# Matmuls of constants into an unused PSUM bank inside the recurrence stage of a two-block transformer kernel

## The reference, cut to what matters

```python
def _gla_scan(q, k, log_f, v, s0):
    ...
    def step(s, xs):
        qc, kc, gc, vc = xs
        a = jnp.cumsum(gc, axis=2)
        diff = a[:, :, :, None, :] - a[:, :, None, :, :]
        decay = jnp.exp(jnp.where(causal[:, :, None], diff, -jnp.inf))
        scores = jnp.sum(qc[:, :, :, None, :] * kc[:, :, None, :, :] * decay, axis=-1)
        o = jnp.einsum('bhts,bhsv->bhtv', scores, vc) + jnp.einsum('bhtk,bhkv->bhtv', qc * jnp.exp(a), s)
        a_last = a[:, :, -1:, :]
        s_new = jnp.exp(a_last[:, :, 0, :, None]) * s + jnp.einsum('bhsk,bhsv->bhkv', kc * jnp.exp(a_last - a), vc)
        return s_new, o
```

## Time and profile before

| what | value |
|---|---|
| runs | 3959.08, 3965.97 and 3971.05 us; median 3965.97 us |
| span of the profiled execution | 3950.7 us, 15.3 us less than the median of the runs |
| PE busy | 3628.5 us, 92% of the span |
| DVE busy | 2203.3 us, 56% |
| ACT busy | 1589.9 us, 40% |
| mean granted TensorE clock | 0.944 |
| chain that ended last, by engine | PE 81%, DVE 8%, ACT 5%, DMA 4%, issue 2% |

### The profile page before, as it was taken

The page is one execution under the profiler, slowest core; times in us unless marked ns, Lnnn a source line. Parts: engine busy times, 40 slices in busy tenths (PEclk is TensorE's granted clock), DMA queues, the critical chain, the costliest instruction groups (busy, mean ns, idle before and its releaser), DMA issues.

```text
span 3950.7 us, 52215 instructions
## 1 busy us (share of the span) xinstructions
PE 3628.5 (92%) x19934; PEld 2784.4 (70%) x19934; DVE 2203.3 (56%) x3277; ACT 1589.9 (40%) x2690; POOL 304.0 (8%) x398
## 2 busy tenths in 40 slices
PE   8998797999999687999999998999999999889998
PEld 7886465666788445456878766787877878667877
DVE  7866855897785784237762346665233332654332
ACT  3335744898423662113222336322233222453222
POOL 0110001110111002001210000111000001000001
PEclk9999568999999758999999999999999999999999
DMA  7551013998455005997773310575323223312222
GB/s 278 175 170 65 2 54 107 347 373 312 173 195 161 1 34 213 409 406 261 267 240 104 101 59 12 186 232 197 105 81 128 96 94 104 134 33 91 93 94 75
DMA packets 164958, 618.35 MB, mean 157 GB/s; under 512 B 18540, under 2 KB 20117, under 8 KB 163581
## 3 DMA queue, kind: packets, MB, share of 16 engines
q1 hardware_dynamic: 114928, 420.58, 29.6%
q0 software_dynamic: 45568, 166.75, 12.8%
q10 hardware_dynamic: 4238, 27.90, 1.8%
HBM read 595.95 MB, written 16.31 MB: 155 GB/s over the span
## 4 chain that ended last, share of the span: by engine, by line
PE 81%; DVE 8%; ACT 5%; DMA 4%; issue 2%; SPq 0%; ACTq 0%; POOL 0%; DVEq 0%; POOLq 0%
PE psum L2500 23%; PE psum L2513 12%; PE psum L843 12%; PE psum L928 5%; PE psum L995 4%; PE psum L2108 4%; DMA ring<-wtile 3%; PE psum L772 3%; PE psum L2339 2%; PE psum L1212 1%; PE psum L2127 1%; PE psum L2358 1%; PE psum L1222 1%; PE psum L780 1%; DVE spare L1318 1%
## 5 line engine op out<-in xcount | busy, mean ns | idle before, releaser
L796 ACT CAST small_r<-ring 128x1024 fp32r<-128x1024 f32 x263 | 275.0, 1048 | 1070.6 <-PE psum L843 336.6
L800 DVE TENSOR_TENSOR ring_r<-ring,small_r 128x1024 fp32r<-128x1024 f32 x264 | 322.8, 1225 | 677.4 <-ACT small_r L796 677.1
L796 ACT CAST PB_r<-ring 128x1024 fp32r<-128x1024 f32 x247 | 255.8, 1049 | 544.2 <-PE psum L2500 326.8
L800 DVE TENSOR_TENSOR ring_r<-ring,PB_r 128x1024 fp32r<-128x1024 f32 x248 | 299.5, 1222 | 247.8 <-ACT PB_r L796 247.4
L2500 PE MATMUL psum<-H_r,ring_r 128*128 128x512 f32 x1344 | 336.3, 392 | 0.0
L2500 PE MATMUL psum<-H_r,small_r 128*128 128x512 f32 x1344 | 326.9, 395 | 0.0
L2500 PE MATMUL psum<-H_r,PB_r 128*128 128x512 f32 x1344 | 318.7, 390 | 0.0
L2500 PEld LDWEIGHTS psum<-H_r,small_r 128*128 128x128 f32 x1344 | 252.4, 188 | 61.1
L2500 PEld LDWEIGHTS psum<-H_r,ring_r 128*128 128x128 f32 x1344 | 252.3, 188 | 55.9
L2500 PEld LDWEIGHTS psum<-H_r,PB_r 128*128 128x128 f32 x1344 | 252.4, 188 | 53.3
L843 PE MATMUL psum<-H_r,small_r 128*128 128x512 f32 (+1 forms) x1040 | 275.2, 368 | 0.1
(11 more groups left out here) (445 smaller groups left out, 6589.7 us busy)
## 6 DMA issues: line engine op xcount, KB each, us to landing
ring<-wtile SPq DMA_DIRECT2D x776, 512.0 KB, 5.3
spare<-wmod POOLq DMA_DIRECT2D x97, 512.0 KB, 4.8
H<-wmod POOLq DMA_DIRECT2D x48, 512.0 KB, 4.5
PB<-wmod POOLq DMA_DIRECT2D x48, 512.0 KB, 4.4
X<-wmod POOLq DMA_DIRECT2D x47, 512.0 KB, 4.9
PB<-wahead POOLq DMA_DIRECT2D x16, 512.0 KB, 7.5
h_rows<-PB POOLq DMA_DIRECT2D x10, 512.0 KB, 4.5
PB<-wmod SPq DMA_DIRECT2D x4, 1024.0 KB, 15.5
```

Of the source, the lines that this page charges most:

```text
L796: copy(high(j), slot(g0 + j)).then_inc(high_ready.sem, 1)
L800: nc.vector.tensor_tensor(low(g0 + j), slot(g0 + j), high(j).bitcast(F32), ALU.subtract).then_inc(low_ready.sem, 1)
```

## The change

A helper `filler` issues matmuls of `ones` against the first columns of `ident` and its neighbour, into bank 7, with no semaphore. It is called at five places on TensorE and nowhere else: 12 matmuls of 256 columns ahead of the first cell's wait, 9 ahead of the wait for the first cell's second piece, 9 ahead of the wait for the second cell; and in every unit of cells 0 to 3 and of units 0 to 3 of cell 4 (28 units) one of 256 columns ahead of `output` and one of 128 columns ahead of `contribution`. That is 86 matmuls in each layer, 172 in all. Nothing is removed, and no wait is added or taken away.

```diff
             def ten(eng):
+                def filler(count, width):
+                    for _ in range(count):
+                        nc.tensor.matmul(bank[7][:, 0:width], ones, cn("ident", 0, width), start=True, stop=True)
+
                 def scores(u):
                     c, v, ch, d, i = units[u]
+                    if (c, v) in ((0, 0), (0, 2), (1, 0)):
+                        filler(12 if v == 0 and c == 0 else 9, 2 * P)
                     if (c, v) == (0, 0):
                         eng.wait_ge(cell_ready.sem, b_ce + 1)
                     if (c, v) == (0, 2) or c and v == 0:
...
                     if u + 1 < n:
                         scores(u + 1)
+                    if c < 4 or (c == 4 and v < 4):
+                        filler(1, 2 * P)
                     output(u)
                     if u + 1 < n:
+                        if c < 4 or (c == 4 and v < 4):
+                            filler(1, P)
                         contribution(u + 1)
```

## The result

The changed kernel takes 4012.3 us (median of 4 runs, 4009.04 to 4017.21) against 3962.5 us for the kernel before beside it. The ratio of the runs is 1.0139, with a 95% interval of 1.0113 to 1.0166 (the two medians alone divide to 1.0126, inside it): slower, and the forecast of 4014 us lies 1.7 us off. The total hides two steps that went another way than foretold, and they cancel.

What follows compares the result with a forecast made beforehand. It took TensorE at 1.2 GHz to bound layer 0's recurrence, narrowly ahead of VectorE, and VectorE layer 1's. Adding +30 and +18 to the 3950.7 us span gave 3998.7, plus 15.3 for the runs' median: 4014 us, range 3942 to 4037.

Steps and rivals of the forecast that it cites:

- The price at the low level: Recurrence units at 1.2 GHz: the two fillers add 1.88 us, making a unit 5.4 us; layer 0 pays it in full.
- VectorE's wait for L1631: Sign that the forecast is right: in the low-clock units VectorE would wait for this line; no size given.
- The clock is lost at the start of the third cell: Layer 0 recurrence: high clock lost there, so 17 units pay 1.88 us each, 32.0 us; forecast's chance 0.47.
- the second rival: Clock lost before the second cell or never raised: 23 units pay, 43 us and 29 us, 4037 us; chance 0.13.
- a unit's middle is safe: Inside units the wide fillers keep the clock high; only passages with output and the narrow filler between stands endanger it.
- once reached, as lasting to the last filler: Both recurrences: the low clock, once reached, stays until the last filler, despite full-array fillers at 1.88 in 5.4 us.
- +18: Layer 1 recurrence: 17 units at 1.25 us, 21.3, less 1 for the first cell and 2 for a recovery.
- the third rival: Clock swings, lost at a cell's start and raised again within a cell: 3966 to 3980, say 3970 us; chance 0.14.
- +30: Layer 0 recurrence: 32.0 us for 17 low-clock units, less 1 and 1 gained, plus 0.2 lost.
- The first and second blocks: Twelve fillers before the first cell give nothing; nine before its second piece take 6 or 7 us, delaying it 0.2.
- The first rival (the clock holds): Clock stays high in both recurrences: 14.3 us gained in layer 0, 5.7 in layer 1, 3946 us; chance 0.26.

Runs made afterwards that it cites:

- with 15 fillers: Changed kernel with 15 instead of 9 fillers ahead of the second cell's wait, in both layers: 3954.1 us, ratio 1.0001.
- the run of layer 1 alone: Changed kernel with all its fillers in layer 1 only, none in layer 0: 3971.6 us, ratio 1.0048.
- kick: Changed kernel plus 9 wide fillers ahead of the third cell's wait in layer 0: 3978.1 us, ratio 1.0061.
- the run of units alone: Changed kernel without the blocks of 12, 9 and 9 fillers, the two fillers of each unit kept: 4027.9 us, ratio 1.0197.

## Why the prediction was right, and where it was not

**The price at the low level: right.** Foretold 1.15 + 0.73 = 1.88 us in a unit of 5.4; measured 1.15 + 0.72 in 5.42. The full price is paid in layer 0: from the second cell's scores to the sixth's it takes 44.3 us more than before, for 23 pairs of fillers (23 x 1.87 = 43.0). VectorE's wait for L1631, named as a sign, came to 3.6 us from 448.5 to 523.5 us; it waited far longer, 24.2 us, for the contribution.

**The place: wrong in both layers.** "The clock is lost at the start of the third cell" failed. It was lost at the second cell's wait, as the second rival had it with 0.13: that rival gave layer 0 43 us, and it cost 191.5 - 150.7 = 40.8 us against the trace that the prediction used. That rival's "2 us standing" (its own sum is 6.20 - 9 x 0.43 = 2.33) was 2.41, and I had set it aside for a stand of 1.2 us that I took for the weaker place. In layer 0 that stand is absent at the third and the fourth cell and 0.71 us at the fifth: a unit of 3.2 us leaves TensorE hardly ahead of VectorE. The weak place was the longer wait, and the row for it was at hand. That "a unit's middle is safe" failed too, in layer 1: with 15 fillers the clock was lost there behind a stand of 1.23 us inside a unit.

**How long it stays low: right in layer 0, wrong in layer 1.** In layer 0 the low level, "once reached, as lasting to the last filler", did so: from 448.4 us past the last filler's end at 566.8 us. In layer 1 it came back at 1482.7 us, after 51 us, where two context units bring the fillers closer; the prediction had named that place and given it 2 us. The two cells at the low level cost 10.7 us (from the second cell's first scores to the fourth's, 1437.51 to 1485.49 us against 1388.13 to 1425.38 before), about 0.9 us a unit where 1.25 was foretold, and what follows them gave back 5.7. In place of +18 (or the rival's +29) layer 1 cost 5.4 us, no more than layers 1 without fillers differ from one another, and 16 in the run of layer 1 alone. There the clock swung, as the third rival had it. So +30 and +18 were +41 and +5: 48 foretold, 46 found in the two recurrences.

**The base was one of two.** The sum was made against one trace, whose layer 0 happened to lack a rise that others have. Against 142.7 us the change costs 48.8 + 5.4 = 54.2 us, and the median of the runs, 4012.3, lies 54.8 us over the 3957.5 us that the kernel before took in a later batch (25 runs). The forecast's 1.7 us from the median are thus partly luck: a loss placed too late, one made too long, and a base 8 us high.

**The first and second blocks.** The twelve give nothing, as foretold: they end at 410.1 us, and TensorE stands 4.76 us before the first cell, at whose start the clock is low (from 414.3 us). The nine took 5.42 us where 6 to 7 were foretold, and the second piece was not late. The second cell's scores come 44.0 us after the attention's end, 44.5 before, a gain of 0.5 where 1 was taken.

**The first rival (the clock holds) was mis-priced.** It gave fillers 0.68 us a unit at the high level by wide matmuls that follow one another; between other tiles they take 1.05. A unit becomes 3.2 us, not 2.9, so the chain that ended last still runs through TensorE, and of the 3 us of VectorE's waits 1.6 come by the fifth cell. The rest of layer 0's gain, 11.5 us against the trace that the prediction used, is mostly made in the last two cells, where the kernel before often has the high clock anyway (against its second trace the whole gain is 3.5). By the runs, with fillers in layer 0 alone, it is 6 us by one ratio and 1 by the other, and the second is not clear of noise; 14.3 were foretold for that layer. The 5.7 us of layer 1 stay untested: no run held the clock there throughout.

## What to carry to other kernels

Filler work on the engine that sets the pace has to be priced at both clock levels and in its place between other tiles, where the wide one cost 0.63 us and not 0.43: if the unit with fillers at the high clock is hardly shorter than the unit without them at the low clock (3.14 against 3.23 us on the average here), there is little to win and 50 us to lose. Look for the longest wait that the filler does not cover to its end, and cover it with a margin or not at all: 12 fillers in place of 15 gave a kernel that is 50 us slower in three runs of ten. And take a second trace of the kernel before, where a stretch at the low clock holds something that could have raised it.

## What was not expected of the hardware

- Both levels can last under the same work. In layer 0 units with fillers stayed at 0.50 for 111.5 us (changed kernel) and at 1.00 for 56 us (kick) and 94 us (15 at the second wait), and nine 128x128 float32 matmuls against 256 columns moved them from the one to the other.
- A full TensorE does not raise the clock by that alone: in the run of units alone it was busy 88.80 of 88.80 us (480.0 to 568.8) at 0.50, with two full-array matmuls in every unit. Which property of the nine does it was not separated.
- A head sum that starts at the low level (2.0 us) raises the clock in two of the three traces without fillers in layer 0 and not in the third, and with a stand that was traced at 1.11 us three runs of ten show the longer time. The Trainium skill, TensorE: Matmul & The Clock Gate, section What's actually happening, says that the number of slow matmuls ahead of a rise varies from run to run; the traces agree and go further: the rise comes or does not come, with 8 us on one layer (142.7 and 150.7).
- A 256-column float32 filler takes 0.43 us behind its like, 0.63 between small tiles at the high level, 1.15 at the low one; the 128-column one 0.42 and 0.72.

Not tried: a longer stand with the same number of fillers ahead of it, fillers in the units behind the last one, narrower fillers than 128 columns, and the twelve first ones taken away alone.
